# Down products of a SwiGLU in seven block products instead of eight, in the last block of rows

## The reference, cut to what matters

```
h2 = _rmsnorm(x, norm2_g)
ff = silu(h2 @ w_ffn_gate) * (h2 @ w_ffn_up)      # 1024 -> 2816
x  = x + ff @ w_ffn_down                          # 2816 -> 1024
return _rmsnorm(x, norm_f_g)
```

## Time and profile before

| | |
|---|---|
| median of the runs | 3198.76 us |
| profiled execution, span from first to last instruction | 3196.7 us |
| PE busy | 3156.0 us (99%) |
| POOL busy | 2036.0 us (64%) |
| DVE busy | 1814.8 us (57%) |
| ACT busy | 1420.8 us (44%) |

### The profile page before, as it was taken

The page is one execution under the profiler, slowest core; times in us unless marked ns, Lnnn a source line. Parts: engine busy times, 40 slices in busy tenths (PEclk is TensorE's granted clock), DMA queues, the critical chain, the costliest instruction groups (busy, mean ns, idle before and its releaser), DMA issues.

```text
span 3196.7 us, 44024 instructions
## 1 busy us (share of the span) xinstructions
PE 3156.0 (99%) x15678; PEld 2655.0 (83%) x15678; DVE 1814.8 (57%) x3706; ACT 1420.8 (44%) x2589; POOL 2036.0 (64%) x2201
## 2 busy tenths in 40 slices
PE   9999999999999999999999999999999999999998
PEld 7888888878878888888888888988888799888887
DVE  3335546537565545557666666967868689521111
ACT  3324435435473534337354534837655378320001
POOL 5666766665556666764666676366767922666676
PEclk9999999999999999999999999999999999999999
DMA  5765455355615333331533334163333500533332
GB/s 152 198 167 172 119 154 157 103 157 163 209 35 182 102 112 107 108 125 57 201 104 116 103 102 138 28 238 103 98 109 112 171 23 17 180 91 99 95 103 99
DMA packets 464201, 392.59 MB, mean 123 GB/s; under 512 B 29264, under 2 KB 394064, under 8 KB 463344
## 3 DMA queue, kind: packets, MB, share of 16 engines
q1 hardware_dynamic: 442544, 345.56, 36.0%
q10 hardware_dynamic: 21440, 44.22, 3.7%
HBM read 323.76 MB, written 62.81 MB: 121 GB/s over the span
## 4 chain that ended last, share of the span: by engine, by line
PE 92%; POOL 2%; ACT 2%; DVE 2%; issue 1%; DMA 1%; SPq 0%; POOLq 0%; ACTq 0%; DVEq 0%
PE BANK L1049 22%; PE BANK L1051 21%; PE BANK L1050 21%; PE LP L1049 4%; PE LP L1051 4%; PE LP L1050 4%; PE BANK L1330 3%; PE BANK L1355 2%; PE LP L1166 2%; PE LP L1165 2%; PE LP L1310 2%; PE LP L1311 2%; PE BANK L1357 2%; POOL WLO L986 1%; POOL WHI L984 1%
## 5 line engine op out<-in xcount | busy, mean ns | idle before, releaser
L986 POOL TENSOR_TENSOR WLO<-WRAW,WHI 128x512 fp32r<-128x512 f32 x912 | 1213.3, 1330 | 76.0
L984 POOL TENSOR_SCALAR WHI<-WRAW 128x512 fp32r<-128x512 f32 x912 | 639.6, 701 | 776.1 <-PE BANK L1051 622.1
L1049 PE MATMUL BANK<-H2hi,WHI 128*128 128x512 f32 x1376 | 538.7, 392 | 1.1 <-POOL WLO L986 1.1
L1050 PE MATMUL BANK<-H2lo,WHI 128*128 128x512 f32 x1376 | 535.9, 389 | 0.0
L1051 PE MATMUL BANK<-H2hi,WLO 128*128 128x512 f32 x1376 | 535.8, 389 | 0.0
L1049 PE MATMUL BANK<-HThi,WHI 128*128 128x512 f32 (+1 forms) x1024 | 405.1, 396 | 0.8 <-DVE QS L2044 0.5
L1050 PE MATMUL BANK<-HTlo,WHI 128*128 128x512 f32 (+1 forms) x1024 | 399.4, 390 | 0.0
L1051 PE MATMUL BANK<-HThi,WLO 128*128 128x512 f32 (+1 forms) x1024 | 399.3, 390 | 0.0
L1751 ACT ACTIVATE MASK<-SCD,THR 128x896 bf16<-128x896 f32 (+5 forms) x186 | 281.9, 1516 | 191.8 <-DVE THR L2104 164.6
L1051 PEld LDWEIGHTS BANK<-H2hi,WLO 128*128 128x128 f32 x1376 | 258.3, 188 | 54.4
L1049 PEld LDWEIGHTS BANK<-H2hi,WHI 128*128 128x128 f32 x1376 | 258.6, 188 | 53.3 <-issue 1.3
(11 more groups left out here) (314 smaller groups left out, 6457.6 us busy)
## 6 DMA issues: line engine op xcount, KB each, us to landing
WRAW<-in_w_in SPq DMA_DIRECT2D x124, 512.0 KB, 4.2
WRAW<-in_w_ffn_gate SPq DMA_DIRECT2D x88, 512.0 KB, 3.8
WRAW<-in_w_ffn_up SPq DMA_DIRECT2D x88, 512.0 KB, 3.8
WRAW<-in_w_ffn_down SPq DMA_DIRECT2D x88, 512.0 KB, 3.5
qsp<-QS SPq DMA_DIRECT2D x32, 512.0 KB, 5.8
WRAW<-in_w_out SPq DMA_DIRECT2D x32, 512.0 KB, 4.6
gates<-GS ACTq DMA_DIRECT2D x62, 256.0 KB, 2.2
GL<-gates ACTq DMA_DIRECT2D x48, 256.0 KB, 4.5
```

The costliest lines, as they stand in the source:

```text
L984: nc.gpsimd.tensor_scalar(hi, raw, 1.0, 1.0, ALU.mult, ALU.mult).then_inc(w_hi, 1)
L986: nc.gpsimd.tensor_tensor(lo, raw, hi.bitcast(f32), ALU.subtract).then_inc(w_split, 1)
L1049: nc.tensor.matmul(dst, whi, mhi, start=first, stop=False)
L1050: nc.tensor.matmul(dst, whi, mlo, start=False, stop=False)
```

## The change

In the last block (`SEVEN`) all three parts make their down product from seven block products. For a pair of tiles (even, odd) and the 512 rows as two halves of 256, the pair's product is a 2 x 2 product of blocks; with sums of blocks it takes seven products and not eight. Each of the seven goes over the part's pairs in two banks (two row tiles of 128), and the banks are accumulated further and added to `X1` after each product (`INTO`), so that the sums of products come about by themselves. In a part of 8 this is 7 x 4 pairs x 2 row tiles x 3 = 168 matmuls, in the part of 6 it is 126.

- The sums of the left side: DVE multiplies the even and the odd tile into `EVEN` and `ODD` in SBUF (and not in PSUM), and makes four differences or sums of 256 columns for each pair, one with the even tile and three with the odd; ACT copies the high parts (`FFhi`, and 768 columns `SThi`), DVE subtracts for the low ones.
- The sums of the right side: for each tile a unit of the raw down weights, half a pair's columns, is loaded by SP once more (`load_unit`, two DMAs of 256 KB into `RQ`), after the unit before has been summed. DVE makes four differences of 256 columns (`sum_unit`); for each pair ACT copies 2 x 1024 columns to `THI`, and DVE subtracts 2 x 1024 into `TLO` (`lower_t`). At the last but one tile of a part, `sum_unit` runs both before and after the tile's own work, and its second unit belongs to the last tile.
- Three of the seven products take raw weights from jobs: 6 jobs for a part, where there were 8, 8 and 6. Four take `THI` and `TLO`. A product waits until the bank that it accumulates in has been added to `X1` (two products before).
- The last product of the last part goes row tile by row tile; it ends with column half 0, and the squares, the mean and the pieces of the final norm have their halves changed about.
- Some semaphores are merged (`ones_set`, `eps_set` and `big_set` into `consts_set`, and others like it); the instructions that count them up and wait are the same.

The core of the diff:

```diff
+SEVEN = (NB - 1,)
+def seven(b, part):
+    return b in SEVEN
+LEFT = ("a11", 0, 1, 2, "s3", "a12", "a22")
+RIGHT = ((0, 0), 0, 1, (1, 1), 2, (1, 0), 3)
+PLACE = (0, 1, 0, 1, 0, 1, 0)
+OPENS = (True, True, False, False, False, True, False)
+INTO = ((0, 0), (1, 1), (0, 1), (0, 1), (1, 1), (0, 0), (1, 0))
+LAST_INTO = {to: m for m, to in enumerate(INTO)}
...
+def turned_after(part, f):
+    last = len(part) - 1
+    return None if f == 0 or f < last and f % 2 else f // 2 if f == last else f // 2 - 1
...
         jobs.append((("fu", b, i), weights(io["w_ffn_up"][0], range(KT), i * P)))
-    return jobs + row_jobs(("fd", part[0]), b, io["w_ffn_down"][0], part)
+    w = io["w_ffn_down"][0]
+    if seven(b, part):
+        return jobs + [(seven_key(b, part, m, a), every_other(w, part, *RIGHT[m], a))
+                       for m in range(7) if type(RIGHT[m]) is tuple for a in range(2)]
...
+    def load_unit(b, part, u):
+        before = (part[0], u - 1) if u else (part[0] - SLOTS, SLOTS - 1)
+        if u or part[0]:
+            sp.wait_ge(t_summed, n(t_summed, (b, *before, 3)))
...
+            i = part[0] + 2 * p + h
+            src = io["w_ffn_down"][0, i * P:(i + 1) * P, :].rearrange("p (d c) -> p d c", d=2)[:, :, c:c + 2 * P]
+            sp.dma_start(RQ[h][:, :, :], src).then_inc(t_in, 16)
...
+        for part in PARTS if b in SEVEN else ():
+            if seven(b, part):
+                for u in range(len(part)):
+                    if key == (("fg", b, part[0]) if u == 0 else ("fu", b, part[u + 1]) if u + 1 < len(part) else seven_key(b, part, 0, 0)):
+                        load_unit(b, part, u)
...
+    def seven_products(b, part):
+        dst = [[take("low", rows_added, added_key(b, part, (6, 5)[place], jj), ("sd", b, part[0], place, jj)) for jj in range(2)]
+               for place in range(2)]
+        for m in range(7):
+            left, right, place = LEFT[m], RIGHT[m], PLACE[m]
+            if m > 1:
+                pe.wait_ge(rows_added, n(rows_added, added_key(b, part, m - 2, 1)))
...
+            rowwise = m == 6 and part is PARTS[-1]
+            for p, jjs in [(p, (jj,)) for jj in range(2) for p in pairs] if rowwise else [(p, range(2)) for p in pairs]:
+                if type(right) is tuple:
+                    if p % 2 == 0:
+                        i = job_no[0]
+                        job_no[0] += 1
+                    pe.wait_ge(w_split, 2 * i + p % 2 + 1)
+                    mhi, mlo = (w[i % 2][:, :, :].rearrange("p (k s) c -> p k (s c)", k=2)[:, p % 2, :] for w in (WHI, WLO))
+                else:
+                    pe.wait_ge(t_low, n(t_low, (b, part[0], p, right // 2)))
+                    mhi, mlo = THI[:, p, right, :], TLO[:, p, right, :]
+                if type(left) is int:
+                    pe.wait_ge(s_low, n(s_low, (b, part[2 * p])))
+                    shi, slo = SThi[:, p, left, :], STlo[p // 2][:, p % 2, left, :]
+                else:
+                    f = 2 * p + (left in ("a12", "a22"))
+                    pe.wait_ge(ff_split, n(ff_split, (b, part[f])))
+                    c = slice(2 * P, 4 * P) if left in ("s3", "a22") else slice(0, 2 * P)
+                    shi, slo = FFhi[:, f, c], FFlo[:, f, c]
+                for jj in jjs:
+                    q = slice(jj * P, (jj + 1) * P)
+                    d, end = dst[place][jj][:, :], p == pairs[-1] and m in (3, 5, 6)
...
+        def seven_high(part, i):
+            f, p = i - part[0], (i - part[0]) // 2
+            if f % 2 == 0:
+                act.wait_ge(s_made, n(s_made, (b, i)))
+                nc.scalar.copy(FFhi[:, f, :].rearrange("p (h r) -> p h r", h=2), EVEN[:, 0:2, :]
+                               ).then_inc(ff_hi, made(ff_hi, (b, i)))
+            else:
+                act.wait_ge(ff_ready, n(ff_ready, (b, i)))
+                nc.scalar.copy(FFhi[:, f, :], ODD[:, :, :].rearrange("p h r -> p (h r)")).then_inc(ff_hi, made(ff_hi, (b, i)))
+                act.wait_ge(s_made, n(s_made, (b, i, 2)))
+                nc.scalar.copy(SThi[:, p, :, :], STR[p // 2][:, p % 2, :, :]).then_inc(s_hi, made(s_hi, (b, part[2 * p])))
+            p = turned_after(part, f)
+            if p is not None:
+                act.wait_ge(t_summed, n(t_summed, (b, part[0], 2 * p + 1, 3)))
+                for t in range(2):
+                    nc.scalar.copy(THI[:, p, 2 * t:2 * t + 2, :], TRAW[:, p, 2 * t:2 * t + 2, :]
+                                   ).then_inc(t_hi, made(t_hi, (b, part[0], p, t)))
         last_square = [None]
...
+        def sum_unit(part, u):
+            p, c = u // 2, slice(u % 2 * 2 * P, (u % 2 + 1) * 2 * P)
+            dve.wait_ge(t_in, n(t_in, (b, part[0], u)))
+            for t, x, y in ((0, RQ[0][:, 1, :], RQ[0][:, 0, :]), (2, RQ[1][:, 1, :], RQ[0][:, 1, :]),
+                            (1, RQ[1][:, 1, :], TRAW[:, p, 0, c]), (3, RQ[1][:, 0, :], TRAW[:, p, 1, c])):
+                if t in (1, 3):
+                    dve.wait_ge(t_summed, n(t_summed, (b, part[0], u, t // 2)))
+                nc.vector.tensor_tensor(TRAW[:, p, t, c], x, y, ALU.subtract
+                                        ).then_inc(t_summed, made(t_summed, (b, part[0], u, (0, 1, 2, 3)[t])))
+        def lower_t(part, p):
+            for t in range(2):
+                dve.wait_ge(t_hi, n(t_hi, (b, part[0], p, t)))
+                nc.vector.tensor_tensor(TLO[:, p, 2 * t:2 * t + 2, :], TRAW[:, p, 2 * t:2 * t + 2, :],
+                                        THI[:, p, 2 * t:2 * t + 2, :].bitcast(f32), ALU.subtract
+                                        ).then_inc(t_low, made(t_low, (b, part[0], p, t)))
+        def seven_low(part, i):
+            f, p = i - part[0], (i - part[0]) // 2
+            bk, gate = bank(("fu", b, i)), SL[:, i % 2, :]
+            if f == len(part) - 2:
+                sum_unit(part, f)
+            full(("fu", b, i))
+            dve.wait_ge(silu_ready, n(silu_ready, (b, i)))
+            if f % 2 == 0:
+                if f:
+                    dve.wait_ge(ff_split, n(ff_split, (b, i - 2)))
+                nc.vector.tensor_tensor(EVEN[:, 0:3:2, :], bk[:, :].rearrange("p (h r) -> p h r", h=2),
+                                        gate.rearrange("p (h r) -> p h r", h=2), ALU.mult).then_inc(ff_ready, made(ff_ready, (b, i)))
+                dve.wait_ge(ff_ready, n(ff_ready, (b, i)))
+                nc.vector.tensor_tensor(EVEN[:, 1, :], EVEN[:, 0, :], EVEN[:, 2, :], ALU.subtract
+                                        ).then_inc(s_made, made(s_made, (b, i)))
+                dve.wait_ge(ff_hi, n(ff_hi, (b, i)))
+                nc.vector.tensor_tensor(FFlo[:, f, :].rearrange("p (h r) -> p h r", h=2), EVEN[:, 0:2, :],
+                                        FFhi[:, f, :].bitcast(f32).rearrange("p (h r) -> p h r", h=2), ALU.subtract
+                                        ).then_inc(ff_split, made(ff_split, (b, i)))
+            else:
+                raw, low = STR[p // 2][:, p % 2, :, :], STlo[p // 2][:, p % 2, :, :]
+                odd = ODD[:, :, :].rearrange("p h r -> p (h r)")
+                if f > 1:
+                    dve.wait_ge(ff_split, n(ff_split, (b, i - 2)))
+                nc.vector.tensor_tensor(odd, bk[:, :], gate, ALU.mult).then_inc(ff_ready, made(ff_ready, (b, i)))
+                dve.wait_ge(ff_ready, n(ff_ready, (b, i)))
+                for k, x, y, op in ((0, EVEN[:, 2, :], ODD[:, 1, :], ALU.add), (1, raw[:, 0, :], EVEN[:, 0, :], ALU.subtract),
+                                    (2, ODD[:, 0, :], raw[:, 1, :], ALU.subtract)):
+                    if k:
+                        dve.wait_ge(s_made, n(s_made, (b, i, k - 1)))
+                    nc.vector.tensor_tensor(raw[:, k, :], x, y, op).then_inc(s_made, made(s_made, (b, i, k)))
+                dve.wait_ge(s_made, n(s_made, (b, i, 2)))
+                dve.wait_ge(ff_hi, n(ff_hi, (b, i)))
+                nc.vector.tensor_tensor(FFlo[:, f, :], odd, FFhi[:, f, :].bitcast(f32), ALU.subtract
+                                        ).then_inc(ff_split, made(ff_split, (b, i)))
+                dve.wait_ge(s_hi, n(s_hi, (b, part[2 * p])))
+                nc.vector.tensor_tensor(low, raw, SThi[:, p, :, :].bitcast(f32), ALU.subtract
+                                        ).then_inc(s_low, made(s_low, (b, part[2 * p])))
+            if f < len(part) - 1:
+                sum_unit(part, f + (f == len(part) - 2))
+            if turned_after(part, f) is not None:
+                lower_t(part, turned_after(part, f))
+        def finish_row(j):
+            dve.wait_ge(rinv_ready, n(rinv_ready, (b, 2, j)))
+            nc.vector.scalar_tensor_tensor(X1[:, j, 0:ROWS], X1[:, j, 0:ROWS], SS[:, j:j + 1], GFB[:, 0:ROWS],
+                                           ALU.mult, ALU.mult).then_inc(y_ready, made(y_ready, (b, j)))
+        def add_products(part, before):
+            seen = {}
+            for m in range(7):
+                i, d = INTO[m]
+                if m == 5 and part is PARTS[-1]:
```

(70 more changed lines are left out.)

89 lines of the change are left out of this document (50 added, 39 removed).

## The result

The changed kernel takes 3209.36 us (median of six runs, 3206.78 to 3212.05); the kernel before, on the same chip, 3199.28 (six, 3197.91 to 3200.22). The ratio is 1.0031, with 95% between 1.0021 and 1.0042: 10 us slower.

A forecast was written before the change was run, and what follows sets the result against it. PE's matmuls were taken to bound the kernel, the chain being 92% PE. The sum was 3196.7 - 15.0 + 21.3 + 1.7 + 1.0 = 3205.7, with 2.06 around it 3207.8, taken as 3207; range 3186 to 3213.

The forecast's parts named there:

- the clock, as a cost of its own: PE's long wait in the part of 6: one fall of the granted clock to half, 1.7 us, between 0 and 5.
- the end: POOL's last splits, products and pieces after PE's end: 1.0 us more, between 0 and 2.
- Part 1: Last block's down products on PE: 66 matmuls fewer at 0.2267 us each, 15.0 us off, all on the path.
- Part 2: DVE beside POOL: instructions with two SBUF inputs take turns with POOL's steps; the form reading PSUM does not.
- the turns: One DVE instruction with two SBUF inputs for one POOL step; 256 columns end 0.28 us after POOL's step.
- Part 3: DVE's work through a part: just keeps up (10.8 of 10.88 us); last tile's multiplication ends 5.6 us after its up job.
- tie breaks: In the taking of turns, these could put each last multiplication some 0.8 us sooner, so 3207 was taken.
- Part 4: PE's waits in the last block's three down products: 6.2, 6.2 and 8.9 us, 21.3 in sum, plus 1.7 for the clock.
- Part 5: The kernel's end on POOL: splits to T + 6.7, products T + 13.5, last pieces T + 16.9; 1.0 us more.
- Contention without lateness: Rival: POOL and DVE take turns, but DVE reaches the last tile on time; 3192.2 us, chance 0.20.
- Hidden: Rival: DVE's added work in the last block is hidden; 3186.0 us, chance 0.16.
- worse: Rival: clock falls in each part and chains are 2 us longer; 3217 us at the outside, chance 0.04.

The follow-up runs named there:

- the two quiet kernels: The changed kernel and the kernel before, each with POOL's split steps in the last block's feed-forward jobs on 8 of 128 columns: 3182.9 and 3197.87 us.
- e1_quiet_before: The kernel before, with POOL's split steps in the last block's feed-forward jobs on 8 of 128 columns: 3197.87 us.
- e3_act_before: The kernel before, with the high parts of the last block's weights copied by ACT in place of POOL's first step: 3198.16 us.
- e2_once: The changed kernel, with only each part's first unit loaded and every unit's differences made from it: 3198.37 us.
- e3_act_after: The changed kernel, with the high parts of the last block's weights copied by ACT in place of POOL's first step: 3194.11 us.
- e1_quiet_after: The changed kernel, with POOL's split steps in the last block's feed-forward jobs on 8 of 128 columns: 3182.9 us.

## Why the prediction was right, point by point

Forecast 3207.0 us with a range of 3186 to 3213, and slower as the likeliest sign; measured 3209.36, so 10.1 us slower where 8.2 were forecast. Against the spans, with which the sum was made, the terms are:

| us | predicted | measured |
|---|---|---|
| matmuls taken away | -15.0 | -15.0 |
| product 2 late, three parts | +21.3 | +22.1 |
| the clock, as a cost of its own | +1.7 | 0 |
| the end | +1.0 | +1.1 |
| behind product 2's start | 0 | +0.4 |
| ahead of the last block's down products | 0 | +0.8 |
| sum | +9.0 | +9.4 |

The mechanism is the predicted one. That the sums agree within 0.4 is partly luck: the clock's term was wrong, and the profiled execution is one of the changed kernel's faster ones.

**Part 1** (66 x 0.2267 = 15.0) holds; the two quiet kernels show it alone.

**Part 2**, the turns, holds: with them gone no lateness is left. But the chained loads are needed for its size: without them 12.2 of the 22.1 us are left. **Part 3**, DVE's line, can be followed in the DVE timeline of the changed kernel, part 2:

```profile
3150.28 0.61 DVE L2660 TENSOR_TENSOR TRAW<-RQ 128x256 f32<-128x256 f32 x1 [3.91 <-DMA RQ<-in_w_ffn_down]
...
3151.93 0.69 DVE L2682 TENSOR_TENSOR EVEN<-BANK,SL 128x512 f32<-128x512 f32 x1
...
3155.89 0.43 DVE L2660 TENSOR_TENSOR TRAW<-RQ 128x256 f32<-128x256 f32 x1 [0.40 <-DMA RQ<-in_w_ffn_down]
3156.23 1.51 DVE L2660 TENSOR_TENSOR TRAW<-RQ,RQ 128x256 f32<-128x256 f32 x1
3157.67 2.26 DVE L2660 TENSOR_TENSOR TRAW<-RQ,TRAW 128x256 f32<-128x256 f32 x2
3159.85 3.85 DVE L2667 TENSOR_TENSOR TLO<-TRAW,THI 128x1024 fp32r<-128x1024 f32 x2
3163.63 0.68 DVE L2696 TENSOR_TENSOR ODD<-BANK,SL 128x512 f32<-128x512 f32 x1
...
3168.91 2.02 DVE L2708 TENSOR_TENSOR STlo<-STR,SThi 128x768 fp32r<-128x768 f32 x1
3170.86 3.84 DVE L2667 TENSOR_TENSOR TLO<-TRAW,THI 128x1024 fp32r<-128x1024 f32 x2
3174.62 2.47 DVE L2733 TENSOR_TENSOR X<-LP,X 128x512 f32<-128x512 f32 x4
```

| step, us after the even (then the last) tile's up job | predicted | measured |
|---|---|---|
| first unit there | 3.7 | 3.8 |
| even tile's multiplication ends | 6.1 | 6.1 |
| second unit there | 9.2 | 9.4 |
| its four sums end | 11.9 | 13.4 |
| last tile's multiplication ends | 5.6 | 6.9 |
| `low` ends | 11.5 | 13.5 |
| last `TLO` ends | 15.3 | 17.3 |
| additions of product 0 end | 16.8 | 18.5 |

(The even tile's up job ends at 3146.5, the last one's at 3157.4.) The loads fit within 0.2 us. The first term that is off is the second unit's four sums: 4.0 us, where I had 2.7, because I let two of them pass POOL untouched (0.4 and 0.3), and in the rows three of the four are drawn out (1.51, and 2.26 for two). Another 0.7 is lost up to `low`. The forecast's "tie breaks", which I let take 0.8 us off, went the other way in this part.

**Part 4.** The lateness that PE saw was predicted at 6.2, 6.2 and 8.9 us, in sum 21.3, and was 4.8, 6.7 and 10.6, in sum 22.1. The places are the predicted ones, except that in part 0 PE didn't wait for `TLO`: DVE and POOL met at other moments there and in part 2. The clock's 1.7 us was a mistake: the fall came, and in part 0 as well (0.60 of full speed in the window from 3168, 0.58 in that from 3174, 0.50 in that from 2924), but both times under DVE's chain, where it costs nothing. I had added a stretch of slow PE to a sum in which DVE is last. The wrong 1.7 us was made good by chance: part 2's chain was 1.7 longer than predicted.

**Part 5.** Counted from product 3's end T (3184.1), the splits end at T + 7.0 (predicted 6.7), the five products at T + 13.7 (13.5), the last piece at T + 17.2 (16.9); the end costs 1.1 us, predicted 1.0. The three last pieces were put at 3.4 us, without a reason, where they took 4.03 before; they took 3.31 (the chain's end in the earlier trace rows against these lines of POOL, changed kernel):

```profile
3191.05 6.73 POOL L1080 TENSOR_TENSOR XH<-X,GFB 128x512 f32<-128x512 f32 x5
3197.96 3.31 POOL L1085 TENSOR_SCALAR X<-XH,SS 128x1024 f32<-128x1024 f32 x3 [0.18 <-POOL XH L1080]
```

**Left out of the sum** was 0.8 us that arises in blocks whose products the change leaves alone. The same windows, first of the changed kernel, then of the one before:

```profile
902.00:904.00 2.00, 2.00 (x13) 1.93 (x13) 1.60 (x9) 1.39 (x8) 2.00 (x5) 0.60 0.01 4
904.00:906.00 2.00, 2.00 (x12) 2.00 (x11) 1.20 (x6) 0.81 (x3) 2.00 (x6) 0.55 0.00 0
```

```profile
902.00:904.00 2.00, 1.57 (x12) 1.43 (x13) 1.68 (x10) 1.42 (x7) 1.49 (x4) 1.00 0.03 9
904.00:906.00 2.00, 2.00 (x17) 1.81 (x17) 1.69 (x9) 1.78 (x7) 2.00 (x6) 1.00 0.00 0
```

In the changed kernel's execution the clock falls here, in the other it doesn't. But this is no trait of the change: in e1_quiet_before and e3_act_before, whose code up to the last block is the kernel before's, it falls as well (0.50 in the window from 904 in both). The last block's first down matmul starts anywhere from 2914.78 (e2_once) to 2918.50 us (e3_act_before) in the ten profiles. The 0.8 us lies within this spread between executions, and no run here charges it to the change.

**The rivals.** "Contention without lateness" (3192.2) fell: DVE was 6.2 us late at the last tile of part 2. e3_act_after, which has half the turns, comes near its number, but with DVE still 4.2 us late at that tile, so the nearness is chance. (Its bound of 7.4 us comes to 7.3 by its own terms.) "Hidden" (3186.0) is near what e1_quiet_after shows, 3182.9, once POOL is out of the way. Of "worse", the longer chain came true in part 2 alone, and the clock fell in two parts, at no cost.
